# Splitting the norm between layers one and two by kind of token, and moving the query's rstd into the exponential

## The reference, cut to what matters

```
x  = x  + gate  * rms_norm(y,  post_g[0])      # end of layer one, image tokens
xc = xc + cgate * rms_norm(yc, post_g[0])      # end of layer one, context tokens
h  = rms_norm(x,  pre_g[1]) * (1 + scale)  + shift
hc = rms_norm(xc, pre_g[1]) * (1 + cscale) + cshift
q  = rope(rms_norm(h  @ w_q, g_q))             # image tokens: queries, 8 heads of 128
k  = rope(rms_norm(h  @ w_k, g_k)),  v = h @ w_v
kc = rms_norm(hc @ w_k, g_k),        vc = hc @ w_v   # context tokens: keys and values only
p  = softmax(q @ concat(k, kc) * 128 ** -0.5)
```

## Time and profile before

| | |
|---|---|
| median of 3 runs | 901.16 us (899.75 to 903.43) |
| profiled execution | 901.08 us, span of its records 898.7 us |
| PE busy | 818.0 us (91% of the span) |
| DVE busy | 498.7 us (55%) |
| ACT busy | 387.6 us (43%) |
| share of PE in the chain that ended last | 72% |
| longest PE waits, by releaser | L741 on DVE's `xn`: 18.1 us in 3 waits; start-up: 14.0 us; L765 on DVE's combined probabilities: 9.8 us in 16 |
| out0 chunk 1 begins, last unit ends | 359.7 us, about 382 us |
| in1 unit (0,0) begins | 396.45 us |

### The profile page before, as it was taken

How to read it: one execution, slowest core, us unless ns; L and a number is a source line. 1 busy time by engine, 2 the same in 40 slices (tenths; PEclk the granted TensorE clock), 3 DMA queues, 4 the chain that set the end, 5 groups by cost and what they waited for, 6 DMA issues and landing times.

```text
span 898.7 us, 10677 instructions
## 1 busy us (share of the span) xinstructions
PE 818.0 (91%) x3999; PEld 630.6 (70%) x3999; DVE 498.7 (55%) x843; ACT 387.6 (43%) x706; POOL 40.5 (5%) x56
## 2 busy tenths in 40 slices
PE   1899999999998999959989987999989899999997
PEld 0577787776666676847757765787767678888886
DVE  2444333225657564688744456688785464654653
ACT  3322221327766754274245354644243344434431
POOL 2200000000001010111100000100010000000000
PEclk9699999999999999979999998999979799999999
DMA  9944553335000071227222033954104254654621
GB/s 324 377 158 141 187 187 141 123 112 186 1 1 1 1 254 38 75 79 273 103 93 94 1 118 122 322 181 135 47 26 165 85 194 146 227 189 148 227 94 47
DMA packets 70085, 121.87 MB, mean 136 GB/s; under 512 B 2602, under 2 KB 28428, under 8 KB 69908
## 3 DMA queue, kind: packets, MB, share of 16 engines
q1 hardware_dynamic: 69188, 118.84, 38.0%
q0 software_dynamic: 560, 1.31, 0.6%
q10 hardware_dynamic: 288, 1.05, 0.3%
HBM read 120.13 MB, written 1.06 MB: 135 GB/s over the span
## 4 chain that ended last, share of the span: by engine, by line
PE 72%; DVE 13%; ACT 6%; issue 4%; DMA 3%; POOL 1%; SPq 1%; DVEq 0%; POOLq 0%; ACTq 0%
PE psum L686 17%; PE psum L688 16%; PE psum L687 16%; DVE w_lo L1593 3%; PE psum L802 2%; PE psum L1085 2%; PE psum L1087 2%; PE psum L1086 2%; PE psum L765 2%; ACT w_hi L1118 2%; DMA act_lo_as_f<-in_ada_w 2%; PE psum L886 2%; PE psum L708 2%; PE psum L878 2%; POOL rstd L1563 1%
## 5 line engine op out<-in xcount | busy, mean ns | idle before, releaser
L686 PE MATMUL psum<-w_hi,act_hi 128*128 128x512 f32 (+1 forms) x752 | 307.3, 409 | 9.4 <-DVE w_lo L1593 3.0
L688 PE MATMUL psum<-w_hi,act_lo 128*128 128x512 f32 (+1 forms) x752 | 295.0, 392 | 0.0
L687 PE MATMUL psum<-w_lo,act_hi 128*128 128x512 f32 (+1 forms) x752 | 294.9, 392 | 0.0
L1593 DVE TENSOR_TENSOR w_lo<-raw,w_hi 128x2048 fp32r<-128x2048 f32 (+1 forms) x83 | 187.8, 2267 | 160.0 <-ACT w_hi L1118 159.9
L1118 ACT ACTIVATE w_hi<-raw 128x2048 fp32r<-128x2048 f32 (+1 forms) x83 | 157.0, 1895 | 124.4 <-PE psum L688 56.5
L686 PEld LDWEIGHTS psum<-w_hi,act_hi 128*128 128x128 f32 x752 | 143.4, 191 | 66.8 <-issue 33.2
L688 PEld LDWEIGHTS psum<-w_hi,act_lo 128*128 128x128 f32 x752 | 142.9, 190 | 30.6
L687 PEld LDWEIGHTS psum<-w_lo,act_hi 128*128 128x128 f32 x752 | 143.3, 191 | 26.7 <-issue 1.2
L1563 POOL TENSOR_TENSOR rstd<-ms,half_neg 128x1 f32<-128x1 f32 (+3 forms) x38 | 33.6, 888 | 637.6 <-DVE ms L1616 637.6
L1248 ACT ACTIVATE sc<-psum,nmax 128x512 f32<-128x512 f32 (+1 forms) x64 | 36.7, 581 | 30.8 <-DVE nmax L1784 30.8
L1784 DVE TENSOR_REDUCE nmax<-psum 128x2 f32<-128x1024 f32 (+1 forms) x32 | 30.5, 956 | 34.8 <-PE psum L802 34.8
(11 more groups left out here) (206 smaller groups left out, 850.9 us busy)
## 6 DMA issues: line engine op xcount, KB each, us to landing
raw<-in_a_w_in SPq DMA_DIRECT2D x16, 1024.0 KB, 9.2
raw<-in_ada_w SPq DMA_DIRECT2D x16, 1024.0 KB, 5.1
raw<-in_w_out SPq DMA_DIRECT2D x12, 1024.0 KB, 5.1
raw<-in_w_gate SPq DMA_DIRECT2D x22, 512.0 KB, 3.8
raw<-in_w_up SPq DMA_DIRECT2D x22, 512.0 KB, 4.9
raw<-in_w_down SPq DMA_DIRECT2D x11, 1024.0 KB, 4.8
raw<-in_b_w_in SPq DMA_DIRECT2D x10, 1024.0 KB, 7.5
raw<-in_w_in SPq DMA_DIRECT2D x10, 1024.0 KB, 9.3
```

Source lines behind the costliest of these rows:

```text
L686: pe.matmul(o[:, 0:n], x_hi, hi[:, kk, :], start=(k == 0), stop=False)
L687: pe.matmul(o[:, 0:n], x_hi, lo[:, kk, :], start=False, stop=False)
L688: mm = pe.matmul(o[:, 0:n], x_lo, hi[:, kk, :], start=False, stop=(k == KT - 1))
L1593: seq.note(dve.tensor_tensor(w_lo[:, at, r], raw[:, at, r], w_hi[:, n % RING, r].bitcast(F32), ALU.subtract).then_inc(s_wlo, 1), s_wlo)
```

## The change

The parts, in the order of the program:

- `out0` chunk 1 takes the tiles in the order 0, 1, 2, 3 instead of 0, 2, 1, 3, and units (1,2) and (1,3) are cut into halves. The transposes of the image tiles' `xn` (16 of them, slices 0 to 3, then 4 to 7) are put between and behind the last half units.
- `xn` of all four tiles is written by ACT (`normed1`) instead of DVE. For the image tiles ACT writes `act_hi` straight from PSUM, and the float copy from which `act_lo` is taken for the even slices; DVE does that copy for the odd ones (`modulated1`, `lo1`).
- Context tile 2's `post_mean` and residual come on DVE after the eight `lo1` of the image tiles, context tile 3's after the first query unit of `in1`.
- The context tiles' transposes (`norm1c`, 16) are put behind units (1,1) and (2,0) of `in1`, into banks 4 and 5 in turn; their `act_hi` and `act_lo` are made at the same places on ACT and DVE. Unit (2,2), the first on a context tile, waits for all of them.
- Query units lose the multiplication with rstd and gain (L1957). The gain is put into the rotation's tables once (four small products), DVE rotates directly out of PSUM, and the rstd is the `scale` of the exponential; DVE multiplies the row maximum with it, one more instruction of 128x1 per step of the attention.

The core of the diff:

```diff
@@ PE
-            for t in TILES0:
-                gemm_unit("out0", 1, t)
-            norm("norm1")
+            gemm_unit("out0", 1, 0)
+            gemm_unit("out0", 1, 1)
+            gemm_unit("out0", 1, 2, FIRST)
+            gemm_unit("out0", 1, 3, FIRST)
+            gemm_unit("out0", 1, 2, SECOND)
+            norm("norm1", FIRST)
+            gemm_unit("out0", 1, 3, SECOND)
+            norm("norm1", SECOND)
...
+                if n < len(units) and units[n] in NORM_IN1:
+                    norm("norm1c", NORM_IN1[units[n]])
@@ banks
+    for k in range(KT):
+        put(("norm1c", k), 4 + k % 2)
@@ ACT
+            out_unit("out0", 1, 0)
+            norm_square("norm1", 0, 0)
+            out_unit("out0", 1, 1)
+            normed1(0)
+            norm_square("norm1", 1, 1)
+            normed1(1)
             split_through(half_no[("in1", 0, 0)] + 1)
-            norm_square("norm1", TILES0[NT - 1], NT - 1)
-            norm_modulated("norm1", 1)
+            out_unit("out0", 1, 2)
+            for k in FIRST:
+                modulated1("norm1", k)
+            out_unit("out0", 1, 3)
+            for k in SECOND:
+                modulated1("norm1", k)
             split_through(half_no[("in1", 0, 0)] + 2)
+            norm_square("norm1", 2, 2)
...
+                if (c, t) == (0, 0):
+                    normed1(2)
+                elif (c, t) == (0, 1):
+                    norm_square("norm1", 3, 3)
+                    normed1(3)
+                for k in NORM_IN1.get((c, t), ()):
+                    modulated1("norm1c", k)
@@ DVE
-            run_chunk("out0", 1, unit_out0, before_norm=True)
-            residual_steps(0, TILES0, NT)
-            residual_steps(0, TILES0, NT + 1)
+            for t in range(XT):
+                post_mean(0, t)
+                residual(0, t)
+                norm_mean("norm1", t)
             split_through(half_no[("in1", 0, 0)] + 1)
-            norm_lo_modulated("norm1", 1)
+            for k in range(KT):
+                lo1("norm1", k)
+            post_mean(0, 2)
+            residual(0, 2)
             split_through(half_no[("in1", 0, 0)] + 2)
+            norm_mean("norm1", 2)
...
+                if c < 2:
+                    rope(psum[:, place[name][0], :], (rope_q[:, 0, t], rope_q[:, 1, t]), w, 64, rot_buf(nm), name)
+                    if (c, t) == (0, 0):
+                        post_mean(0, 3)
+                        residual(0, 3)
+                    elif (c, t) == (0, 1):
+                        norm_mean("norm1", 3)
+                    elif t:
+                        gates1(0)
+                    for k in NORM_IN1.get((c, t), ()):
+                        lo1("norm1c", k)
+                    return
@@ attention of layer two
-                seq.note(dve.tensor_reduce(nmax[:, p % 2, 0:1], psum[:, b, :], AX_X, ALU.max, negate=True).then_inc(s_mx, 1), s_mx)
+                m = nmax[:, p % 2, 0:1]
+                seq.note(dve.tensor_reduce(m, psum[:, b, :], AX_X, ALU.max, negate=True).then_inc(s_v, 1), s_v)
+                dve.wait_ge(*seq.last)
+                seq.note(dve.tensor_scalar(m, m, query_rstd(p), None, ALU.mult).then_inc(s_mx, 1), s_mx)
```

More of the change, by code:

```diff
@@ L65 @@
 GATE_IN1 = {(1, 0): 0, (2, 1): 1}
+NORM_IN1 = {(1, 1): range(0, 4), (2, 0): range(4, 8)}
 def loads_plan():
@@ L98, in gemm_tiles @@
     if stage == "out0":
-        return TILES0
+        return [0, 1, 2, 3] if chunk else TILES0
     if stage == "in0" or (stage, chunk) == ("in1", 2):
@@ L495, in block_kernel @@
                            + [(("sub", t), 8) for t in TILES0]
-                           + residual_pows(0, TILES0)
-                           + [(("qk1", c, t), 4 if c < 2 else 2) for c in range(3) for t in gemm_tiles("in1", c)]
+                           + [((name, t), 1) for t in range(3) for name in ("post0", "norm1")]
+                           + [(("qk1", 0, 0), 4), (("post0", 3), 1), (("qk1", 0, 1), 4), (("norm1", 3), 1)]
+                           + [(("qk1", c, t), 4 if c < 2 else 2) for c in (1, 2) for t in gemm_tiles("in1", c)]
                            + residual_pows(1, range(XT))
@@ L606, in tile_cols, with features1, query_rstd @@
             return slice(t * P, (t + n) * P)
+        def features1(stage, k):
+            return sc[:, 4 + k % 4, 0:XT * P] if stage == "norm1" else v_flat[:, 2048 + XT * P * (k % 4):2048 + XT * P * (k % 4 + 1)]
+        def query_rstd(p):
+            t, h = divmod(p, HEADS)
+            n0 = pow_at[("qk1", h // 4, t)][1] + h % 4
+            return rstd[:, n0:n0 + 1]
         def feature_no(stage, t):
@@ L1327, in _, with normed1 @@
[L1327 to L1331 removed]
+            def normed1(t):
+                act.wait_ge(s_powout, pow_at[("norm1", t)][0] + 1)
+                n0 = pow_at[("norm1", t)][1]
+                act.activation(xn[:, t, :], xs[:, t, :], ACTF.Copy, scale=rstd[:, n0:n0 + 1]).then_inc(s_xn1, 1)
@@ new lines, in modulated1 @@
+            def modulated1(stage, k):
+                s, last = (0, ("out0", 1, 1)) if stage == "norm1" else (1, ("out0", 1, 3))
+                act.wait_ge(s_mod, 3 + k // HALF_KT)
+                act.wait_ge(*finished(last))
+                act.wait_ge(*finished((stage, k)))
+                ps = psum[:, place[(stage, k)][0], 0:XT * P]
+                scale, bias = mod[:, 1, 0, k, s:s + 1], mod[:, 1, 1, k, s:s + 1]
+                seq.note(act.activation(act_hi[:, k, XT * P * s:XT * P * (s + 1)], ps, ACTF.Identity, scale=scale,
+                                        bias=bias).then_inc(s_h, 1), s_h)
+                if stage == "norm1" and k % 2:
+                    return
+                if k >= 4:
+                    act.wait_ge(s_act, act_base[stage] + k - 3)
+                seq.freed(act.activation(features1(stage, k), ps, ACTF.Identity, scale=scale, bias=bias)
+                          .then_inc(bank_free((stage, k)), 1), (stage, k))
@@ L1627, in norm_in @@
                 tiles = norm_tiles[stage]
-                for t in range(tiles):
+                for t in tiles:
                     squares((stage, t))
@@ L1677, in rope @@
                 cos, sin = table
-                full_cos = cos.unsqueeze(1).unsqueeze(1).broadcast_to((P, heads, 2, half))
-                one_sin = sin.unsqueeze(1).broadcast_to((P, heads, half))
+                if len(cos.shape) == 3:
+                    full_cos = cos.unsqueeze(1).broadcast_to((P, heads, 2, half))
+                    sins = [sin[:, s].unsqueeze(1).broadcast_to((P, heads, half)) for s in range(2)]
+                else:
+                    full_cos = cos.unsqueeze(1).unsqueeze(1).broadcast_to((P, heads, 2, half))
+                    sins = [sin.unsqueeze(1).broadcast_to((P, heads, half))] * 2
                 x, ta, tb, o = v(src), v(sc[:, 3, :]), v(sc[:, 4, :]), v(dst)
```

78 lines of the change are left out of this document (46 added, 32 removed).

## The result

The changed kernel takes 908.86 us in the median of 6 runs (907.0 to 911.97), the kernel before 901.31 us (899.75 to 903.89, 6 runs): a ratio of 1.0083, 95% interval 1.0056 to 1.0111. It is slower by 7.6 us; 6.2 were forecast. The profiled execution of the changed kernel took 911.97 us (span 909.9), the longest of its six together with one other, so its trace has more to explain than the median.

The account below looks back on a forecast made before the run. PE, busy 91% of the span, was taken as the bound. An earlier unit (0,0) (-7.55) against bank waits, clock, transposes and attention summed to +6.2 on 901.1: 907.3 us; range 900.5 to 911.5, leaving out 2 in 10.

Parts of the forecast that it names:

- part 2: Before in1 unit (0,0): PE waits 5.0 us for bank 0 instead of 8.8; the unit begins 7.55 us earlier.
- its length: In1 unit (0,0): 7.2 us instead of 6.69, including 1.7 for half clock after the wait; +0.5 us.
- part 3: Before in1 unit (0,1): PE waits 3.55 us for bank 1, held until tile 3's post_mean; start at 401.5.
- clock behind it: In1 unit (0,1): half clock after the wait for bank 1; +1.7 us.
- part 4: Behind in1 units (1,1) and (2,0): 16 context transposes, +1.8 us, and waits for two banks ACT reads out, +4.7.
- clock behind the context slices: Behind the context transposes' stop of 2.4 + 0.7 us: clock may halve a third time, half of 1.7; +0.85 us.
- waits that went: Before 426.13 and 439.49: two waits of 0.90 and 0.41 us disappear as DVE loses the rstd product; -1.3 us.
- part 5: Attention: extra multiplication of the maximum (0.19) and longer exponential (0.09), 0.28 us in seven odd steps; +1.95 us.
- Rival A: At the later two stops: bank wait stays but the clock does not fall; 904.7 us, chance 0.14.
- Rival B: Before unit (0,0): bank 0 is free in time, by DVE's order; 900.6 or 895.9 us, chance 0.09.
- Rival C: In1: ACT becomes the bound, late weight halves make unit (2,0) wait 4.2 us; 911.5 us, chance 0.14.

Follow-up runs that it names:

- Both: Changed kernel with VectorE's post_mean of tile 2 before the eight context multiplications and of tile 3 before unit (0,0)'s rotation; 898.12 us, ratio 0.9952.
- tile2: Changed kernel with only tile 2's post_mean moved ahead of the context split's half-step and eight context multiplications on VectorE; 904.14 us, ratio 1.0031.
- swap: The spread kernel with ScalarE, in odd attention steps, moving the turned probabilities before the next step's exponential; 891.4 us, ratio 0.9886.
- warm: The swap kernel with three extra matmuls of kT put in each of TensorE's two short stops behind the attention; 890.92 us, ratio 0.9889.
- query: Kernel before with only the change's query part: rotation straight from PSUM, rstd as exponential scale, maximum multiplied by it; 900.58 us, ratio 0.9989.
- spread: The Both kernel with the context norm's eight slices in four pairs, two of them mid-unit, instead of two groups of four; 892.16 us, ratio 0.9895.
- fill: Changed kernel with 19 and 13 extra matmuls keeping TensorE busy in its waits before units (0,0) and (0,1); 904.43 us, ratio 1.0035.
- noscale: Changed kernel without the query's rstd: no scale in the exponential, no multiplication of the maximum; 906.85 us, ratio 1.0052.
- queryswap: The query kernel with ScalarE, in odd attention steps, moving the turned probabilities before the next step's exponential; 901.62 us, ratio 0.9999.
- shift: Kernel before with 8 extra matmuls (1.82 us) ahead of the projection's last unit; 904.75 us, ratio 1.0047.

## Why the prediction was right

By its own steps, the sum up to the first scores:

| term | forecast | measured |
|---|---|---|
| begin of (0,0) (part 2) | -7.55 | -7.74 |
| its length (8.15 against 6.69) | +0.5 | +1.46 |
| wait for bank 1 (part 3) | +3.55 | +3.47 |
| clock behind it (lead 2.73 to 0.18) | +1.7 | +2.55 |
| transposes and two banks (part 4) | +6.5 | +6.8 |
| clock behind the context slices | +0.85 | +1.6 |
| waits that went | -1.3 | -1.3 |
| first scores | +4.25 | +6.8 by the terms, +6.59 in the trace |
| attention (part 5) | +1.95 | +2.43 |

The mechanism was right in its steps: the two banks, in the order named, within 0.8 us of the times named (388.71 for 388.9, 402.26 for 401.5); the longest context stop 2.34 for 2.4; no wait of (2,0) for the weights; the longer exponential 0.09. "Both", which removes exactly the two bank waits, turned the loss of 7.6 us into a gain of 3.2. The transposes and banks are the rows from the end of the modulation part (424.97) to unit (2,0) (427.71), and from the end of (2,0) (433.27) to (2,1) (437.75), less what lies there in the kernel before without its wait: 6.8 us, of which 4.3 are the four waits (4.7 forecast) and 2.5 the sixteen transposes, where I had 1.8. The clock behind them is unit (2,1), 7.15 us long against 5.57.

What was mis-sized is the clock. I charged 1.7 us behind each of the two stops, from the 3.6 us at 0.50 in the earlier trace rows. In the kernel before the clock had fallen 6.5 us before the transposes began:

```profile
381.90:384.40 2.50, 0.18 (x1) 0.00 (x0) 0.65 (x3) 2.10 (x5) 0.09 (x1) 1.00 1.00 380
384.40:390.90 6.50, 0.01 (x1) 0.04 (x1) 5.10 (x11) 3.84 (x5) 2.46 (x4) 0.50 0.33 128
```

At the shorter stops of 4.81 and 3.47 us it fell about 1.4 us before the unit began, and more of the low stretch lay in the work. The units ran 5.3 and 5.4 us slowly, which costs 2.6 us each. The length of the stop does not decide it by itself: in tile2 a stop of 4.28 us was followed by a unit of 7.15 us, only 1.6 us too long. Rival A, no fall at the later stops, is refuted by the windows at 401 and 438. Rival B needed the order of "tile2", which the kernel doesn't have; its price for bank 0 alone, 6.7 us, was too high (4.7 measured): I had left out that the wait for bank 1 grows when (0,0) gets faster (0.8 us), and 1.0 us more went to the low clock at the first scores. Rival C did not happen: ScalarE is busy 44% and (2,0) begins behind its slices, without a wait for `w_lo`. In the chances, the forecast's share of "slower" is 0.45 (0.50 less 0.05), not 0.47; the sum of 0.60 stands.

In the attention I had counted 0.28 us in seven odd steps, as a weight load that waits 0.77 + 0.28 us. It waits 1.11:

```profile
477.88 0.69 DVE L2077 TENSOR_REDUCE nmax<-psum 128x1 f32<-128x512 f32 x1 [3.71 <-PE psum L905]
...
478.90 0.78 ACT L1430 ACTIVATE sc<-psum,nmax,rstd 128x512 f32<-128x512 f32 x1 [4.06 <-issue]
...
480.31 0.97 PEld L913 LDWEIGHTS psum<-vbuf,sc 128*128 128x128 f32 x8 [1.11 <-ACT sc L1217]
480.31 1.16 PE L913 MATMUL psum<-vbuf,sc 128*128 128x128 f32 x8 [0.28 <-ACT sc L1217]
```

The weight load waits 0.34 us more than before, and the pair of an even and an odd step around it grew by 0.36 (from 7.32 to 7.68 us). The 0.28 of the last row counts only the time in which no matmul runs. From the start of the maximum to that of the exponential it is 1.02 us here (477.88 to 478.90) where the earlier trace rows have 0.78: the product adds 0.24, not 0.19, and the exponential 0.09.

The trace of one execution says +10.9, the median +7.6. 1.6 of it is the clock at 731.9. What the other runs of the changed kernel did there isn't recorded, only that their mean clock was 0.966 to 0.970 where the profiled one's was 0.957. The terms as the trace has them add up to 9.3 us; that the median lies no more than 1.4 us above the forecast is in part luck, and where the other runs save the rest is open.

## What to carry to other kernels

When an instruction is moved, look for what it frees as well as for what it computes: here two reads of PSUM were put behind work that looked urgent, and held TensorE's next two units. A stop of TensorE can cost more than its length in the clock behind it (here 2.6 us behind stops of 4.8 and 3.5, and 1.6 behind one of 4.3). And before a gain of 1 to 2 us in one stage is believed, read the clock in the windows of the stages behind it; the best version here (0.9886 and 0.9889 of the kernel before) had its gain already with the orders that removed stops altogether (0.9895), and the medians show nothing more from the two later edits (swap and warm). Last, count from a row ahead of the change before start times of two traces are compared: here the traces lie up to 2.3 us apart before any edit begins.

## What the chip showed that was not expected

- Behind the attention, with the same first stop of 1.7 us and the unit 4.03 us after it, the units ran at 1.00 in the profiled runs of query, both, spread, fill and tile2, and began at 0.50 in those of before, after, noscale, swap, queryswap and shift. The stretch took 15.4 us in the first and 17.0 to 17.45 in the others. In tile2 the clock was low in the transposes (0.50 from 523.2 to 525.9) and back at 1.00 for the unit.
- Keeping TensorE busy in the two stops behind the attention kept the clock at 1.00 there, and the work around two later stops, the first of them unchanged (2.18 us), then ran slower (window at 640.5: 0.51 instead of 0.70).
- At the first scores the clock was low ahead of them in query, tile2 and shift and not in the kernel before or the changed one, behind the same stop of 3.47 us. It cost 0.6 us in query and 1.0 in tile2.
- The 1.89 us stop near 722 us, which cost nothing in the earlier trace rows, cost 1.6 us in the changed kernel's profiled run, and the clock fell behind it in two more of the thirteen profiled kernels.
